# The recurrence's triangular inverse as two diagonal 64x64 blocks, the crossing step last, the pairs of heads written out

## The chip, the cores and the metric

The kernel runs on one core of a Trainium2 chip (trn2). Its engines are TensorE (matrix products, into the accumulator memory PSUM), VectorE, ScalarE, GpSimd and SyncE; in the profile PE, PEld (TensorE's weight loads), DVE, ACT, POOL and SP. They run beside each other and wait for each other through semaphores. The metric is the device time of one execution, in microseconds (us). All data is float32.

## The reference

Two networks in a row, on 256 tokens of width 1024. The change touches one step of the second one, the scan in its RWKV-7 mixer, which runs for 16 heads of width 64, forwards and backwards in time:

```python
def rwkv7_scan(r, w, k, v, kk, a):
    def step(state, inp):
        r_t, w_t, k_t, v_t, kk_t, a_t = inp
        sa = jnp.einsum('bhvk,bhk->bhv', state, -kk_t)
        state = (state * w_t[:, :, None, :] + sa[..., None] * (kk_t * a_t)[:, :, None, :]
                 + v_t[..., None] * k_t[:, :, None, :])
        return state, jnp.einsum('bhvk,bhk->bhv', state, r_t)
    ...
    _, out = lax.scan(step, jnp.zeros((nB, H, N, N), F32), xs)

    dir_out = []
    for d in range(2):
        ...
        o = rwkv7_scan(*ins)
        bonus = jnp.sum(rh * kd * r_k.astype(F32), axis=-1, keepdims=True) * vh
        dir_out.append((group_norm(o, gn_w, gn_b) + bonus.reshape(nB, S, D)) * g.astype(F32))
    y = dir_out[0] + dir_out[1]
```

`sa` of a token depends on the `sa` of all tokens before it. Over a chunk of 128 tokens that is a linear system whose matrix is the unit matrix plus a strictly triangular one, and the kernel solves it by inverting that matrix.

## The kernel before

The function `Rwkv.chunks` (from L2288 on) holds the whole recurrence. It works on pairs of heads: eight pairs, each 128 channels wide, `i` = 0 to 7. Within a pair there are two directions `d`, two chunks `t` of 128 tokens and two heads `hh`; the four matrices of one direction are numbered `n` = 2t + hh. Each direction has four banks of PSUM, `ps[:, 4 * d + 0..3, :]`. Every engine has its own program `pair(i)`, and `all_pairs` (L2347) writes the first and the last pair out and puts the six between into a loop (`Fori`), where slices are addressed and semaphores awaited through registers. Semaphores are named in `N`, and `wait(eng, name, i, k)` waits for the k-th signal of pair i.

A pair goes through these steps:

- *Products* (L2468, L2471). TensorE multiplies the scaled keys (`KR`, part of the tiles `used`) with `Bs` and `Ks`. VectorE multiplies the results by the masks `keep` and writes `GM` (L2673, eight instructions of 128x512); its part `GM[d][:, n, 0]` is the triangular matrix, transposed.
- *M1* (L2478) is the same matrix not transposed, from four more matmuls in a direction, masked by VectorE (L2681).
- *Inversion*. `Xi` is the inverse, `XT` its transpose, both 128x128 and at first the unit matrix (ScalarE, L2413, L2414). There are seven levels (`LEVELS`); level k doubles the size of the inverted diagonal blocks from 2^k. Level 0 is a masked copy of M1 into `Xi` and of GM into `XT` (L2687, L2688; `level` holds the places as 0 or 1). In levels 1 to 6 TensorE does the half step, `P = GM' Xi` (L2488), for both directions; ScalarE copies it out of PSUM (L2422, `Pb`, the same memory as `M1`, printed as M); TensorE makes `XT' P` (L2505) and `P' XT` (L2507); VectorE copies the new places of both (L2701, L2702). The last level makes only `XT`.
- *Gates*. In level 4 (`GATES_AT`) TensorE also makes the gates and the bonus (L2496, L2497), between the half step and the products.
- *State*. TensorE makes the right side `rhs`, ScalarE copies it (L2438), `XT' rhs` is `sa` (all these through `by_halves`, L136, in tiles of 128x64), then the chunk's state (L2538) and outputs. VectorE scales the state into `S0` (L2710), and the second chunk goes the same way. ScalarE copies the outputs `o` (L2450) and the next pair's `used` (L2409), on which the next pair's products wait.

VectorE and ScalarE do more beside the inversion, in an order that is written out. At the start of level 1, 2 and 3 VectorE runs two pieces of `output(i - 1)` (group norm and gates of the pair before, L2626 to L2658), at the start of level 4, 5 and 6 one piece of `factors(i + 1)` (L2580 to L2610, with the exponentials `exps` of ScalarE between), and the last piece after level 6, before it scales the state. GpSimd copies `v` into `vc` once in each pair (L2387), as soon as the pair before has ended.

## Time and profile before

| | us |
|---|---|
| median of 3 runs (3013.49 to 3015.53) | 3014.8 |
| the profiled execution | 3018.51 |
| its span, from the first to the last instruction | 3016.8 |
| TensorE busy | 2778.6 (92%) |
| VectorE busy | 784.0 (26%) |
| ScalarE busy | 420.1 (14%) |
| the mean granted clock of TensorE | 0.965 of 2.4 GHz |

The profile is one execution, recorded by instruction. Times in its views are counted from the start of the span. A float32 matmul stands in it as two records, each with a weight load of its own. A record's own duration contains the way through the array, so the pace of a group is read from the distance of starts. "PEclk" or the granted clock is 1.00 at 2.4 GHz and 0.50 at 1.2 GHz. The recurrence lies between 2282 and 2729 us.

### The profile page before, as it was taken

The numbers are of one execution on the slowest core, as the hardware profiler recorded it, in microseconds if no ns is written. First come the engines' busy times: TensorE is split into PE (matmuls) and PEld (weight loads), VectorE is DVE, ScalarE is ACT, GpSimd is POOL, SyncE is SP. The second block draws the span as 40 slices with busy tenths as digits, with TensorE's granted clock in tenths as the row PEclk, the third lists the DMA queues.
The fourth block names the chain that finished last, engine by engine and source line by source line (L and its number), as shares of the span: only waits on it lengthen the run. The fifth ranks groups of instructions, "written<-read, shape, count | busy, mean of one in ns | idle before, by whom it ended". The sixth has DMA issues, their size and how long they took to land. (4 is left out here: it accounts for less than half of the span.)

```text
span 3016.8 us, 73080 instructions
## 1 busy us (share of the span) xinstructions
PE 2778.6 (92%) x32601; PEld 2324.4 (77%) x32601; DVE 784.0 (26%) x1979; ACT 420.1 (14%) x927; POOL 84.5 (3%) x144
## 2 busy tenths in 40 slices
PE   8899999989889999999999977999998898897998
PEld 7677776768789999899899765666686788786665
DVE  5412000630211101101101112100426777873001
ACT  1101000111110101101001112100123323221000
POOL 0100000010000000000000000000000000001000
PEclk9899999989989999999999997999998999999999
DMA  7334445433379999999999930644410000001442
GB/s 216 112 127 133 147 152 161 136 98 112 147 303 407 407 407 407 407 407 407 407 407 407 319 126 21 187 152 158 152 56 4 3 2 3 2 2 64 153 153 97
DMA packets 291365, 571.04 MB, mean 189 GB/s; under 512 B 18182, under 2 KB 181764, under 8 KB 291284
## 3 DMA queue, kind: packets, MB, share of 16 engines
q1 hardware_dynamic: 291284, 569.92, 52.3%
q8 instruction: 56, 0.92, 0.1%
q14 instruction: 25, 0.20, 0.0%
HBM read 568.79 MB, written 5.28 MB: 190 GB/s over the span
## 5 line engine op out<-in xcount | busy, mean ns | idle before, releaser
L1737 PE MATMUL ps<-xg,ring 128*64 128x80 f32 x14336 | 519.6, 234 | 7.2 <-issue 2.2
L1737 PEld LDWEIGHTS ps<-xg,ring 128*64 128x64 f32 x14336 | 507.1, 138 | 18.0 <-DMA ring<-in_moe_w_up_dram 8.3
L1332 PE MATMUL ps<-xT,ring 128*128 128x256 f32 x1728 | 379.8, 379 | 6.1 <-PEq L452 3.0
L1332 PEld LDWEIGHTS ps<-xT,ring 128*128 128x128 f32 x1728 | 328.3, 190 | 67.0 <-issue 22.4
L1344 PE MATMUL ps<-ring,hidden 128*128 128x512 f32 x688 | 301.8, 592 | 0.0
L1753 PE MATMUL ps<-hidden,expert_down 128*64 128x80 f32 x7168 | 259.5, 233 | 9.2 <-DVE hidden L1829 4.8
L1753 PEld LDWEIGHTS ps<-hidden,expert_down 128*64 128x64 f32 x7168 | 251.9, 137 | 14.8 <-DVE hidden L1829 6.3
L1344 PEld LDWEIGHTS ps<-ring,hidden 128*128 128x128 f32 x688 | 130.9, 190 | 147.3 <-issue 145.3
L618 PE MATMUL ps<-ring,xT 128*128 128x256 f32 (+1 forms) x1056 | 228.3, 379 | 7.4 <-PEq L1213 4.1
L618 PEld LDWEIGHTS ps<-ring,xT 128*128 128x128 f32 x1056 | 198.6, 196 | 36.2 <-issue 9.7
L618 PE MATMUL ps<-xT,ring 128*128 128x256 f32 (+1 forms) x944 | 214.9, 390 | 10.2 <-PEq L596 4.5
L618 PEld LDWEIGHTS ps<-xT,ring 128*128 128x128 f32 (+1 forms) x944 | 178.1, 190 | 44.8 <-issue 14.8
L1829 DVE TENSOR_TENSOR hidden<-acted,ps 128x320 f32<-128x320 f32 x64 | 28.6, 446 | 676.2 <-PE ps L1737 676.2
L1392 DVE TENSOR_TENSOR hidden<-acted,ps 128x512 f32<-128x512 f32 x43 | 29.6, 688 | 605.2 <-ACT acted L1369 397.5
L2488 PE MATMUL ps<-Xi,GM 128*128 128x128 f32 x768 | 116.2, 298 | 18.8 <-DVE Xi L2687 8.9
L2488 PEld LDWEIGHTS ps<-Xi,GM 128*128 128x128 f32 x768 | 99.9, 203 | 32.7 <-DVE Xi L2701 19.8
L1791 ACT ACTIVATE acted<-ps 128x320 f32<-128x320 f32 x64 | 22.4, 401 | 627.0 <-PE ps L1737 627.0
L1369 ACT ACTIVATE acted<-ps 128x512 f32<-128x512 f32 x43 | 25.7, 597 | 598.5 <-PE ps L1332 598.5
L2507 PE MATMUL ps<-XT,M 128*128 128x128 f32 x768 | 102.9, 279 | 0.0
L2507 PEld LDWEIGHTS ps<-XT,M 128*128 128x128 f32 x768 | 95.6, 196 | 0.3
L2505 PE MATMUL ps<-M,XT 128*128 128x128 f32 x640 | 89.6, 286 | 0.0
L2422 ACT ACTIVATE M<-ps 128x512 f32<-128x512 f32 x96 | 57.3, 597 | 218.6 <-PE ps L2488 218.6
(361 smaller groups left out, 2455.9 us busy)
## 6 DMA issues: line engine op xcount, KB each, us to landing
ring<-in_moe_w_gate_dram SPq DMA_DIRECT2D x128, 896.0 KB, 16.6
ring<-in_moe_w_up_dram SPq DMA_DIRECT2D x128, 896.0 KB, 16.7
expert_down<-in_moe_w_down_dram SPq DMA_DIRECT2D x96, 1024.0 KB, 17.3
ring<-in_mlp_w_dram SPq DMA_DIRECT2D x64, 1024.0 KB, 5.7
ring<-in_w_xkv_dram SPq DMA_DIRECT2D x16, 1024.0 KB, 5.2
expert_down<-in_moe_w_down_dram SPq DMA_DIRECT2D x32, 512.0 KB, 16.5
ring<-in_ffn_w_gate_dram SPq DMA_DIRECT2D x11, 1024.0 KB, 5.4
ring<-in_ffn_w_up_dram SPq DMA_DIRECT2D x11, 1024.0 KB, 5.3
```

Of the source, the lines that this page charges most:

```text
L618: mm = pe.matmul(bank(n, dst), left(here), right(here), start=(i == 0), stop=(i == len(pairs) - 1))
L1332: mm = pe.matmul(bank[:, m * SEQ:(m + 1) * SEQ], w[:, c, m * P:(m + 1) * P], self.xT[:, c, :], start=(c == 0), stop=(c == KC - 1))
L1344: mm = pe.matmul(ps[:, 4 + 2 * t + half, :], hidden[:, p, f, t * P:(t + 1) * P], w[:, f, half * 512:(half + 1) * 512], start=first and f = ...
L1369: act.activation(acted[:, p, :], gb[p], ACT.Silu if up else ACT.Relu).then_inc(s["act_done"].sem, 1)
L1392: dve.tensor_tensor(hidden[:, p].rearrange("p f s -> p (f s)"), acted[:, p, :], ub[p], ALU.mult).then_inc(s["hidden_ready"].sem, 1)
L1737: mm = pe.matmul(bank[b][o:o + HEAD, at, :], w[:, c, f * P + o:f * P + o + HEAD], xg[:, p * E_STEP + c, :], start=(p == 0 and c == 0 and a ...
L1753: mm = pe.matmul(yT[c // 4][o:o + HEAD, c % 4, :], w[:, j, c * P + o:c * P + o + HEAD], hidden[:, f, :], start=False, stop=False, skip_gro ...
L1829: dve.tensor_tensor(hidden[:, part, :], acted[:, part, :], src, ALU.mult).then_inc(hidden_ready, 1)
L2422: act.activation(Pb[d][:].rearrange("p a b -> p (a b)"), ps[:, 4 * d, :], ACT.Copy).then_inc(q["half_ready"].sem, 1)
L2488: mm = pe.matmul(ps[:, 4 * d, n * P:(n + 1) * P], GM[d][:, n, 0, :], Xi[d][:, n, :], start=True, stop=True)
L2505: pe.matmul(ps[:, 4 * d + 1, n * P:(n + 1) * P], XT[d][:, n, :], Pb[d][:, n, :], start=True, stop=True)
L2507: mm = pe.matmul(ps[:, 4 * d + 2, n * P:(n + 1) * P], Pb[d][:, n, :], XT[d][:, n, :], start=True, stop=True)
```

## The change

- The inverse is held as its two diagonal blocks of 64x64. `XX[d]` [P, 4, 2, 64] has in the upper 64 partitions the first block and in the lower 64 the second, `XX[.., 0, :]` the inverse and `XX[.., 1, :]` its transpose. `LEVELS` is 6. Each matmul of the inversion becomes two, one for each block `b`, with rows, columns and output in the half `b`: tiles of 64x64 on the diagonal of the array.
- `M1` is made by 16 matmuls of 64x64 in a direction (both kinds, plain and transposed, of both blocks). ScalarE copies it and turns the sign; VectorE's masked multiplication is gone. What lies outside the places is not used.
- One masked copy of 128x512 in a level and direction serves both `XX` parts. ScalarE's copies of the half step have 256 columns.
- A crossing step joins the blocks at the end: four matmuls in a direction (`L2530` of the new kernel), a copy by ScalarE into `PI`, which has unit matrices beside it, four matmuls with 64x128 weights (L2536), a copy by VectorE into `XB`.
- `sa` takes the first half from a 64x64 tile of `XX` and the other from a 128x64 tile, `XB`.
- The third piece of `factors(i + 1)` runs after the last level, ahead of the copy of `XB`.
- All eight pairs are written out; there is no loop.

```diff
-LEVELS = 7
+LEVELS = 6
@@ all_pairs
-            pair(0, first=True)
-            with eng.Fori(1, pairs - 1) as i:
-                pair(i)
-            pair(pairs - 1, last=True)
+            for i in range(pairs):
+                pair(i, first=i == 0, last=i == pairs - 1)
@@ ScalarE
-                        act.activation(Xi[d][:], m.ident[:].unsqueeze(1).to_broadcast([P, 4, P]), ACT.Copy)
-                        act.activation(XT[d][:], m.ident[:].unsqueeze(1).to_broadcast([P, 4, P]), ACT.Copy).then_inc(q["x_begun"].sem, 1)
+                        act.activation(XX[d][:].rearrange("p n k e -> p (n k) e"), eyes[:].unsqueeze(1).to_broadcast([P, 8, HEAD]), ACT.Copy).then_inc(q["x_begun"].sem, 1)
                     for d in range(2):
+                        wait(act, "m1_done", i, d + 1)
+                        act.activation(M1[d][:].rearrange("p t h e -> p h t e"), ps[:, 4 * d:4 * d + 2, 0:4 * HEAD].rearrange("p h (t e) -> p h t e", t=TT),
+                                       ACT.Copy, scale=-1.0).then_inc(q["m1_ready"].sem, 1)
...
-                            act.activation(Pb[d][:].rearrange("p a b -> p (a b)"), ps[:, 4 * d, :], ACT.Copy).then_inc(q["half_ready"].sem, 1)
+                            act.activation(Pb[d][:].rearrange("p a b -> p (a b)"), ps[:, 4 * d, 0:4 * HEAD], ACT.Copy).then_inc(q["half_ready"].sem, 1)
...
+                    for d in range(2):
+                        wait(act, "cross_done", i, d + 1)
+                        to, other = half(1 - d), half(d)
+                        act.activation(PI[to, :, other], ps[to, 4 * d, 0:4 * HEAD].rearrange("p (n e) -> p n e", n=4), ACT.Copy).then_inc(q["cross_ready"].sem, 1)
                     if not last:
                         exps(i + 1, 1)
@@ TensorE
-                                mm = pe.matmul(ps[:, 4 * d + hh, t * P:(t + 1) * P], KR[d][half(hh), t, 0, :], Bs[d][half(hh), t, :], start=True, stop=True)
+                            for kind in range(2):
+                                for b in range(2):
+                                    for hh in range(2):
+                                        a, e = KR[d][half(hh), t, 0, half(b)], Bs[d][half(hh), t, half(b)]
+                                        at = (2 * t + kind) * HEAD
+                                        mm = pe.matmul(ps[half(b), 4 * d + hh, at:at + HEAD], e if kind else a, a if kind else e, start=True, stop=True)
...
                             for n in range(4):
-                                mm = pe.matmul(ps[:, 4 * d, n * P:(n + 1) * P], GM[d][:, n, 0, :], Xi[d][:, n, :], start=True, stop=True)
+                                for b in range(2):
+                                    h = half(b)
+                                    mm = pe.matmul(ps[h, 4 * d, n * HEAD:(n + 1) * HEAD], GM[d][h, n, 0, h], XX[d][h, n, 0, :], start=True, stop=True)
...
-                            if k < LEVELS - 1:
-                                for n in range(4):
-                                    pe.matmul(ps[:, 4 * d + 1, n * P:(n + 1) * P], XT[d][:, n, :], Pb[d][:, n, :], start=True, stop=True)
                             for n in range(4):
-                                mm = pe.matmul(ps[:, 4 * d + 2, n * P:(n + 1) * P], Pb[d][:, n, :], XT[d][:, n, :], start=True, stop=True)
+                                for kind in range(2):
+                                    for b in range(2):
+                                        h = half(b)
+                                        xt, p = XX[d][h, n, 1, :], Pb[d][h, n, :]
+                                        at = (2 * n + kind) * HEAD
+                                        mm = pe.matmul(ps[h, 4 * d + 1, at:at + HEAD], p if kind else xt, xt if kind else p, start=True, stop=True)
                             mm.then_inc(q["step_done"].sem, 1)
+                    for d in range(2):
+                        wait(pe, "x_ready", i, 2 * (LEVELS - 1) + d + 1)
+                        to, other = half(1 - d), half(d)
+                        for n in range(4):
+                            mm = pe.matmul(ps[to, 4 * d, n * HEAD:(n + 1) * HEAD], GM[d][other, n, 0, to], XX[d][other, n, 0, :], start=True, stop=True)
+                        mm.then_inc(q["cross_done"].sem, 1)
+                    for d in range(2):
+                        wait(pe, "cross_ready", i, d + 1)
+                        to = half(1 - d)
+                        for n in range(4):
+                            mm = pe.matmul(ps[:, 4 * d + 1, n * HEAD:(n + 1) * HEAD], PI[to, n, :], XX[d][to, n, 1, :], start=True, stop=True)
+                        mm.then_inc(q["block_done"].sem, 1)
...
                             for hh in range(2):
-                                mm = by_halves(pe, ps[:, 4 * d + 1, hh * HEAD:(hh + 1) * HEAD], XT[d][:, 2 * t + hh, :], rhs[d][:, hh, :], start=True, stop=True)
+                                cols, n = slice(hh * HEAD, (hh + 1) * HEAD), 2 * t + hh
+                                pe.matmul(ps[first_half, 4 * d + 1, cols], XX[d][first_half, n, 1, :], rhs[d][first_half, hh, :], start=True, stop=True)
+                                mm = pe.matmul(ps[other, 4 * d + 1, cols], XB[d][:, n, :], rhs[d][:, hh, :], start=True, stop=True)
@@ VectorE
-                            if lv < LEVELS - 1:
-                                dve.copy_predicated(Xi[d][:], ..., ps[:, 4 * d + 1, :]...).then_inc(q["xi_ready"].sem, 1)
-                            dve.copy_predicated(XT[d][:], ..., ps[:, 4 * d + 2, :]...).then_inc(q["x_ready"].sem, 1)
+                            dve.copy_predicated(whole(XX[d][:]), places(d, lv), ps[:, 4 * d + 1, :].rearrange("p (n e) -> p n e", n=4)).then_inc(q["x_ready"].sem, 1)
+                    beside(after, 1)
+                    for d in range(2):
+                        wait(dve, "block_done", i, d + 1)
+                        dve.tensor_copy(XB[d][:].rearrange("p n e -> p (n e)"), ps[:, 4 * d + 1, 0:4 * HEAD]).then_inc(q["block_ready"].sem, 1)
                     beside(after, 2)
```

How TensorE's program changes, first pair, from the last transpose before the inversion through level 1. Rows give the line, the operation, output and inputs, the output's shape and a count of matmuls; `M_214` and `M_215` are the half steps of the two directions. Before:

```order
L2481 MATMUL ps<-ident,Ks 128x128
L2488 MATMUL ps<-Xi,GM 128x128 x8
L2505 MATMUL ps<-M_214,XT 128x128 x4
L2507 MATMUL ps<-XT,M_214 128x128 x4
L2505 MATMUL ps<-M_215,XT 128x128 x4
L2507 MATMUL ps<-XT,M_215 128x128 x4
```

and of the changed kernel:

```order
L2495 MATMUL ps<-ident,Ks 128x128
L2504 MATMUL ps<-XX,GM 64x64 x16
L2523 MATMUL ps<-Pb,XX 64x64 x2
L2523 MATMUL ps<-XX,Pb 64x64 x2
L2523 MATMUL ps<-Pb,XX 64x64 x2
L2523 MATMUL ps<-XX,Pb 64x64 x2
```

Eight matmuls of the half step became sixteen smaller ones, and the sixteen of the products thirty-two (the two L2523 rows stand eight times in a level).

TensorE again, first pair, the end of the inversion and the first product with `rhs`. Before:

```order
L2488 MATMUL ps<-Xi,GM 128x128 x8
L2507 MATMUL ps<-XT,M_214 128x128 x4
L2507 MATMUL ps<-XT,M_215 128x128 x4
L136 MATMUL ps<-vc,GM 64x64 x8
L136 MATMUL ps<-rhs,XT 64x64 x8
L2538 MATMUL ps<-sa,rowsBK 64x64 x2
```

and of the changed kernel:

```order
L2530 MATMUL ps<-XX,GM 64x64 x8
L2536 MATMUL ps<-XX,PI 128x64 x8
L136 MATMUL ps<-vc,GM 64x64 x8
L2559 MATMUL ps<-rhs,XX 64x64
L2560 MATMUL ps<-rhs,XB 64x64
```

The seventh level went, the two parts of the crossing step came, and the product with `rhs` alternates between two kinds of tiles.

VectorE at the same place. Before:

```order
L2597 TENSOR_TENSOR Y<-X,ring 128x256
L2702 COPY_PREDICATED XT<-level,ps 128x512 x2
L2599 TENSOR_SCALAR fa<-ring,cc 128x256
L2600 SCALAR_TENSOR_TENSOR kd<-fa,k 128x256
L2601 TENSOR_TENSOR bb<-xT,ring 128x256
```

and of the changed kernel:

```order
L2727 COPY_PREDICATED XX<-level,ps 128x512 x2
L2623 SCALAR_TENSOR_TENSOR S<-ones,ring 128x128 x2
L2626 COPY MT<-S 128x2
L2627 TENSOR_TENSOR MT<-S 128x2
L2628 TENSOR_TENSOR X<-S 128x256
L2630 TENSOR_TENSOR Y<-X,ring 128x256
L2731 COPY XB<-ps 128x256 x2
L2632 TENSOR_SCALAR fa<-ring,cc 128x256
```

The third piece of the next pair's factors (up to Y) stood ahead of the last level's copies and stands behind them now, and `XB` lies between it and the fourth piece.

## Rows read from the trace of the kernel before

**Rows 1.** Groups of instructions, 2250 to 2800 us: busy us, mean ns | idle before, releasers.
```profile
L2701 DVE COPY_PREDICATED Xi<-level,ps 128x512 f32<-128x512 int32 x80 | 58.2, 728 | 59.8 <-PE ps L2507 56.5 <-DVE Ks L2610 2.1 <-DVE XT L2702 1.0
```

**Rows 2.** Timeline, level 2 of pair 2: start us, us, engine, instruction [idle before <-releaser].
```profile
2416.53 0.97 PEld L2488 LDWEIGHTS ps<-Xi,GM 128*128 128x128 f32 x8
...
2417.74 0.60 ACT L2422 ACTIVATE M<-ps 128x512 f32<-128x512 f32 x1 [4.99 <-PE ps L2488]
...
2422.66 0.73 DVE L2701 COPY_PREDICATED Xi<-level,ps 128x512 f32<-128x512 int32 x1 [0.32 <-PE ps L2507]
...
2423.44 0.97 PEld L2488 LDWEIGHTS ps<-Xi,GM 128*128 128x128 f32 x8 [1.07 <-DVE Xi L2701]
```

**Rows 3.** Timeline of GpSimd: its copy of v at the start of a pair.
```profile
2344.30 0.40 POOL L2387 COPY vc<-v 128x256 f32 x1 [61.54 <-PE ps L136]
...
2455.33 0.40 POOL L2387 COPY vc<-v 128x256 f32 x1 [41.10 <-PE ps L136]
...
2510.16 0.40 POOL L2387 COPY vc<-v 128x256 f32 x1 [40.68 <-PE ps L136]
...
2563.37 0.40 POOL L2387 COPY vc<-v 128x256 f32 x1 [39.06 <-PE ps L136]
...
2670.35 0.40 POOL L2387 COPY vc<-v 128x256 f32<-128x256 f32 x1 [38.96 <-PE ps L136]
```

**Rows 4.** Timeline: small tiles, and a copy of 256 columns.
```profile
2397.29 0.40 PE L136 MATMUL ps<-vc,GM 128*64 128x64 f32 x8
...
2397.52 1.00 PE L136 MATMUL ps<-rhs,XT 128*64 128x64 f32 x16
...
2399.25 0.38 ACT L2450 ACTIVATE o<-ps 128x256 f32<-128x256 f32 x1 [0.41 <-PE ps L136]
...
2403.91 0.71 PE L2478 MATMUL ps<-Bs,used 64*128 64x128 f32 x8
...
2404.56 0.33 PE L2481 MATMUL ps<-ident,Bs 128*128 128x128 f32 x1
```

**Rows 5.** VectorE by stretches: stretch, its length, busy (x), PEclk, DMA share, GB/s.
```profile
2410.48:2412.63 2.15, 1.84 (x17) 0.50 0.00 0
2418.28:2422.35 4.07, 3.66 (x13) 1.00 0.00 0
2425.12:2428.21 3.09, 2.90 (x13) 1.00 0.00 0
2438.40:2441.61 3.21, 2.93 (x9) 1.00 0.00 0
2444.40:2446.19 1.79, 1.72 (x7) 1.00 0.00 0
2284.35:2287.35 3.00, 2.93 (x9) 0.50 0.01 4
```

**Rows 6.** Timeline of VectorE: state of pair 2, GM of pair 3.
```profile
2450.79 1.43 DVE L2710 TENSOR_SCALAR S<-ps,used 64x64 f32<-64x64 f32 x4
2456.63 4.88 DVE L2673 TENSOR_TENSOR GM<-ps,keep 128x512 f32<-128x512 f32 x8 [4.41 <-PE ps L2471]
```

**Rows 7.** Stretches, all engines: length, PE, PEld, DVE, ACT, POOL, PEclk, DMA, GB/s.
```profile
2405.00:2406.00 1.00, 0.00 (x0) 0.00 (x0) 1.00 (x3) 0.38 (x1) 0.00 (x0) 1.00 0.00 0
2408.00:2409.00 1.00, 1.00 (x5) 1.00 (x6) 1.00 (x3) 0.00 (x0) 0.00 (x0) 0.50 0.00 0
```

**Rows 8.** Timeline: the first GM products, the last matmul of the recurrence.
```profile
2292.02 4.87 DVE L2673 TENSOR_TENSOR GM<-ps,keep 128x512 f32<-128x512 f32 x8
...
2722.68 0.29 PE L136 MATMUL ps<-vc,GM 128*64 128x64 f32 x4
```

**Rows 9.** Timeline and stretches in an earlier stage, around 950 us.
```profile
948.61 1.34 PE L1712 MATMUL ps<-zeros 1*128 1x320 f32 x4
...
949.00:950.00 1.00, 1.00 (x5) 0.48 (x4) 0.41 (x1) 0.00 (x0) 0.00 (x0) 1.00 1.04 414
950.00:951.00 1.00, 1.00 (x12) 0.67 (x13) 0.42 (x1) 0.00 (x0) 0.00 (x0) 0.51 1.01 400
```

64 lines of the change are left out of this document (30 added, 34 removed).

## The prediction

> **What bounds the kernel now.** The change touches one stage, the recurrence of the last mixer: eight pairs of heads in a row, 2288 to 2723 us of a span of 3016.8 us. I read its groups of instructions first [rows 1]. Before VectorE's masked copies (L2701) there are 59.8 us idle, 56.5 of them for the matmuls of L2507. So TensorE is what the inversion waits for. The timeline of one level says the same [rows 2]: 8 weight loads of 128 columns take 0.97 us, about 0.11 each with the matmul behind it. A level has 8 for each of three products in each of two directions, 48 x 0.111 = 5.3 us, and the level shown lasts from 2416.53 to 2423.44 = 6.9 us, since VectorE's other work (below) held it up. Of a pair, the length is read from GpSimd, which copies v once in each [rows 3]: pairs 1 to 6 take (2670.35 - 2344.30) / 6 = 54.3 us, the shortest, 2510.16 to 2563.37, 53.2.
>
> **What a 64x64 tile costs.** No row has one. The nearest are the 128x64 tiles behind L136 [rows 4]: 8 instructions start within 2397.29 to 2397.52, 0.029 us each, two tiles of the array working side by side. Tiles of 64 rows do that too: L2478, 64 rows by 128 columns, has 8 in 0.71 us with the last one's 0.27, some 0.06 each instead of 0.11. The new code alternates the two diagonal quadrants, which differ in rows and in columns. I take 0.029 us. The bounds: 0.025 (the same row, no better) and 0.058, if the two quadrants do not overlap.
>
> **One level, after.** Instructions in a direction: 8 matmuls, 16 records, for the half step (0.46 us), 16 matmuls, 32 records, for the two products (0.93). Both directions: 2.8 us instead of 5.3. But a level is also a chain. ScalarE's copy of the half step has 256 columns and not 512, 0.38 us [rows 4] instead of 0.60 [rows 2]; VectorE's copies are one of 512 instead of two, 0.73 [rows 2]. An engine takes up a finished copy 0.05 us later (2422.66 + 0.73 to 2423.44). For one direction: 0.46 + 0.22 (the last record, as 0.40 less seven starts in rows 4) + 0.05 + 0.38 + 0.05 + 0.93 + 0.22 + 0.05 + 0.73 + 0.05, about 3.2 us. Levels that are alone therefore last 3.2 us, not 2.8.
>
> **And VectorE has other work in them.** It finishes the pair before (levels 1 to 3) and prepares the next (from level 4), and I took the length of each piece from the trace [rows 5]: 2.15, 4.07, 3.09 us, then 3.21 and 1.79; the last piece, as long as the fourth, takes 2.9 from 2447.88 to the row at 2450.79 [rows 6]. Two masked copies follow each piece, 0.62 + 0.73 = 1.35 us with the pipelining that the rows show. This is the new bound. I count a middle pair from K, the end of the eight GM products, to the next K; that of pair 3 is 2456.63 + 4.88 = 2461.51 [rows 6], 6.2 us behind its copy of v at 2455.33 [rows 3], and I use the same 6.2 for the others.
> - Level 0: TensorE's first products M1 are now 16 matmuls in a direction (0.93 us) instead of 4, and ScalarE copies them (0.60) where VectorE multiplied by the mask. VectorE is rid of that multiplication, but waits for the second direction: copies end at K + 2.6.
> - Level 1: 2.15 + 1.4: K + 6.2. Level 2: 4.07 + 1.35: K + 11.6. Level 3: 3.09 + 1.35: K + 16.0.
> - Level 4: here TensorE has the gates as well (8 matmuls of 128 columns, 1.8 us), and it is the bound: K + 21.2.
> - Level 5: 3.21 + 1.35: K + 25.75. There is no level 6.
> - Behind it: 1.79 us of the next pair's work, K + 27.55. Meanwhile the crossing step runs: 8 records for each direction in one quadrant (0.46), ScalarE's copy (0.38), 8 records with 64x128 weights (0.9, as L2488 with its 128 columns). It is ready about when VectorE is, so XB ends at K + 28.4; then 2.9 us: the state's scaling begins at K + 31.3.
> - From there to the next K: 2461.51 - 2450.79 = 10.7 us [rows 6], unchanged except for the product with rhs: it now alternates 64x64 and 128x64 tiles. Changing the tile's shape costs something like the step from L2478 to L2481 (0.71 us of records, 0.27 of them the last's, and 0.65 until the next shape starts [rows 4]: 0.1 more than its pace). Four in each direction are 0.8 us.
> - The loop is written out: VectorE's pieces have register work in it. The fourth piece takes 3.00 us in the first pair, which is straight code already, and 3.21 in the loop [rows 5]; with 0.1 to 0.2 for a piece I take 0.7 off a pair. What else it costs (more instructions to be fetched) I put at nothing: the last pair is straight code as well, and L136 keeps its pace there.
>
> Sum: 31.3 + 10.7 + 0.8 - 0.7 = 42.1 us, if the clock stays at 2.4 GHz.
>
> **The clock.** In the middle of a pair TensorE falls to 1.2 GHz: from 2405 to 2406 it had nothing to do, from 2408 on the granted clock is 0.50 [rows 7], for some microseconds, in six of the eight pairs. Of the six middle ones four have it, and the mean is 1.1 us above the shortest, which has none [rows 3]: 1.7 us for one. After the change TensorE has larger gaps: 2.8 us of work in levels of 4.4 to 5.4, and about 2 us of nothing before VectorE frees the crossing step's followers. At 1.2 GHz a level needs 2 x 2.8 = 5.6 us, and a fall that lasts one to two levels costs about 2.3 us at the start of the pair and some 2.5 at its end (cross and block steps twice as long, with the state behind them). I take 0.75 of the first, 0.4 of a fall in levels 2 and 3 (1.5) and 0.6 of the last: 3.8 us. A middle pair: 42.1 + 3.8 = 45.9, a gain of 8.4.
>
> **The ends.** Pair 0, from K = 2292.02 + 4.87 = 2296.9 [rows 8] to pair 1's at 2344.30 + 6.2 = 2350.5, takes 53.6. It has no pair before it, so levels 1 to 3 take 3.2 us each; by the same steps 27.3 + 11.5 + 3 = 41.8, a gain of 11.8. Pair 7 has nothing to prepare: from K = 2670.35 + 6.2 to the last matmul (2722.68 + 0.29, rows 8) 46.4 us; after, 16.0 at level 3, 21.2 at 4, 24.4 at 5 (3.2 more), 1.9 for the crossing (0.38 + 0.9 + the copy and the waits between), 6.2 for the rest as from the last masked copy to the end now, 0.8 and 2 for the clock: 35.3, a gain of 11.1. All else (loads of tables, the copies of the unit matrices) lies far ahead or beside idle engines. Together 6 x 8.4 + 11.8 + 11.1 = 73.3 us. The profiled execution took 3018.5 us (its span 3016.8), so 2945.2; the median of the runs is 3.7 us lower: **2941 us**.
>
> **A rule against it.** L2478's two row halves write different banks of PSUM. The new diagonal quadrants write one bank, in different partitions; no row shows row tiles doing that. The Trainium skill, TensorEngine Tiling (Array Packing), Restrictions and Gotchas, says of this that "Different row tiles cannot access same PSUM bank simultaneously". By that rule 0.058 us would hold, and the time would be that of the first rival, 3006 us, instead of 2941; the trace has no row that bears it out or speaks against it.
>
> **Rivals.**
> - *No overlap on the diagonal.* 0.058 us an instruction makes a level 96 x 0.058 = 5.6 us, what it is now. One level less and the half of the last save 2.7, the crossing step and M1 give it back: a pair of about 53.4 against 54.3, seven or eight us in all, and the last pair as before: 3006 us; with 1 us either way in a pair, 2998 to 3014.
> - *The clock stays low (slower).* Other rows speak for it: the slice from 949 to 950 is all busy, first with a tile of one row (L1712, 1x128), and so is the next, but its clock is 0.51 [rows 9]. So what the tile covers may count, and 64x64 tiles, two at a time, cover half the array. The Trainium skill, TensorE: Matmul & The Clock Gate, Part 1, speaks of how busy the engine has been recently; by that alone slices of 1.00 would have kept 2.4 GHz, and this rival would have no ground. Against it: 128x64 tiles in rows 4 ran at full clock, with the array full. If the inversion runs at 1.2 GHz from K to the state's scaling, levels take 5.7 us, the gates 3.6, the crossing step 5.4: 43 us instead of 31.3, the tail 12.5: 55.5 against 54.3. Pairs 0 and 7 lose 2 and 1.5: about +10 us, 3025. It decides from the point where more than about 80% of the inversion is at 1.2 GHz.
> - *The instructions are not there in time.* A pair in straight code has about 790 matmul records, twice that with the weight loads. Were each matmul late by 0.01 us where TensorE bounds, a fifth of them, 1.6 us a pair and 13 us in all would go: 2954 us. The last pair shows no such gap, so I give it little.
>
> **Chances.** Forecast 0.70 (2913 with no fall at all, 8 x 3.5 us less; 2981 with two falls more, 5 us, in every pair); no overlap 0.09; low clock 0.17 (3005 to 3045); the rest 0.04. The range 2908 to 3018 takes in the first, nearly all of the second and the low edge of the third. A measurement of this kernel can tell about 0.2%, 6 us, from no change: faster 0.75, within 0.07 (half of no overlap, the edge of the low clock), slower 0.18.
>
> **What would show it.** In the profile after: the spacing of L2523's records (0.029 right, 0.058 the first rival); VectorE busy most of a pair (above 0.8) and TensorE idle for it in levels 1 to 3, with GpSimd's copies of v 42 to 48 us apart; level 4 alone bound by TensorE; one fall of the clock more in each pair at the crossing step. Wrong it would be if the granted clock were 0.5 through most of the inversion, or if L2559 and L2560 cost more than 0.5 us in a direction.

## The result and the profile after

The changed kernel takes 2949.7 us (median of 4 runs, 2943.2 to 2952.2) where the kernel before takes 3015.2 beside it: a ratio of 0.978, 95% interval 0.9763 to 0.9797. Forecast were 2941 us, in a range of 2908 to 3018. The profiled execution took 2948.8 us (span 2947.0), 69.7 less than the 3018.5 of before; the forecast from it was 73.3.

Three groups of the page after. The columns are as in [rows 1]: busy us, mean ns of one | idle time before, and what ended it.

```profile
L2504 PE MATMUL ps<-XX,GM 64*64 64x64 f32 x1280 | 54.8, 228 | 29.4 <-DVE XX L2727 23.5
L2523 PE MATMUL ps<-Pb,XX 64*64 64x64 f32 x1280 | 80.6, 224 | 0.0
...
L2504 PEld LDWEIGHTS ps<-XX,GM 64*64 64x64 f32 x1280 | 44.7, 137 | 39.4 <-DVE XX L2727 30.0
```

Before, VectorE's masked copy waited 56.5 us for TensorE [rows 1]. The group that answers to it, VectorE from 2250 to 2800 us after, waits 28.6:

```profile
L2727 DVE COPY_PREDICATED XX<-level,ps 128x512 f32<-128x512 int32 x80 | 55.8, 722 | 32.2 <-PE ps L2523 28.6 <-DVE Ks L2643 1.2 <-DVE o L2674 1.2
```

Most of what is left of that wait is level 4, with the gates: the two copies of pair 1 there, below, wait 1.92 + 0.20 us; eight times that is 17 us. In the other direction TensorE's half step now waits 23.5 us for VectorE. Both waits are there, and in different levels, as the prediction had it.

GpSimd's copy of v, as in [rows 3], at the start of pairs 1 and 7:

```profile
2332.75 0.40 POOL L2389 COPY vc<-v 128x256 f32<-128x256 f32 x1 [50.44 <-PE ps L136]
...
2609.48 0.40 POOL L2389 COPY vc<-v 128x256 f32<-128x256 f32 x1 [33.51 <-PE ps L136]
```

(2609.48 - 2332.75) / 6 = 46.1 us for a middle pair, against 54.3 before and 45.9 forecast. Now pair 1 in VectorE's timeline (start, us, instruction; as in [rows 6]):

```profile
2334.16 4.87 DVE L2706 TENSOR_TENSOR GM<-ps,keep 128x512 f32<-128x512 f32 x8 [6.06 <-PE ps L2481]
...
2343.29 1.55 DVE L2727 COPY_PREDICATED XX<-level,ps 128x512 f32<-128x512 int32 x2
2348.74 1.34 DVE L2727 COPY_PREDICATED XX<-level,ps 128x512 f32<-128x512 int32 x2 [0.17 <-DVE o L2674]
2352.90 1.33 DVE L2727 COPY_PREDICATED XX<-level,ps 128x512 f32<-128x512 int32 x2
2358.08 0.73 DVE L2727 COPY_PREDICATED XX<-level,ps 128x512 f32<-128x512 int32 x1 [1.92 <-PE ps L2523]
2359.02 0.73 DVE L2727 COPY_PREDICATED XX<-level,ps 128x512 f32<-128x512 int32 x1 [0.20 <-PE ps L2523]
2362.80 1.33 DVE L2727 COPY_PREDICATED XX<-level,ps 128x512 f32<-128x512 int32 x2 [0.17 <-DVE Ks L2643]
...
2366.84 0.42 DVE L2731 COPY XB<-ps 128x256 f32<-128x256 f32 x1 [0.47 <-PE ps L2536]
2371.58 0.70 DVE L2738 TENSOR_SCALAR S<-ps,used 64x64 f32<-64x64 f32 x2 [1.40 <-PE ps L2571]
...
2380.58 4.87 DVE L2706 TENSOR_TENSOR GM<-ps,keep 128x512 f32<-128x512 f32 x8 [7.02 <-PE ps L2481]
```

K is 2334.16 + 4.87 = 2339.03. Read off against the prediction's own marks, in us behind K; the last column is pair 1 of the experiment "fill" below, whose clock never falls (its rows stand there):

| end of | forecast at full clock | after, pair 1 | fill, pair 1 |
|---|---|---|---|
| level 1 | 6.2 | 5.8 | 5.8 |
| level 2 | 11.6 | 11.1 | 11.1 |
| level 3 | 16.0 | 15.2 | 15.2 |
| level 4 | 21.2 | 20.7 | 20.8 |
| level 5 | 25.75 | 25.1 | 25.2 |
| XB | 28.4 | 28.2 | 27.9 |
| state's scaling begins | 31.3 | 32.6 | 30.8 |
| next K | 42.1 | 46.4 | 42.7 |

Up to XB the pair is as drawn. From there to the next K it takes 18.2 us (46.4 - 28.2), where 13.7 were drawn at full clock and fill has 14.8. Two views show why. First the product that gives sa, TensorE's timeline of pair 2, at half clock (step 0, for the first chunk: the first three rows) and at full clock (step 1, for the second: the last three, with the very last record):

```profile
2414.74 0.47 PE L2559 MATMUL ps<-rhs,XX 64*64 64x64 f32 x2
2415.15 0.47 PE L2560 MATMUL ps<-rhs,XB 128*64 128x64 f32 x2
2415.55 0.47 PE L2559 MATMUL ps<-rhs,XX 64*64 64x64 f32 x2
...
2421.46 0.33 PE L2559 MATMUL ps<-rhs,XX 64*64 64x64 f32 x2
2421.72 0.33 PE L2560 MATMUL ps<-rhs,XB 128*64 128x64 f32 x2
...
2423.36 0.22 PE L2560 MATMUL ps<-rhs,XB 128*64 128x64 f32 x1
```

Two records of one shape, then the other shape: 0.257 us each time at full clock, 0.40 at half. Eight of these are a step of both directions: 2.06 or 3.2 us, where its 16 records at 0.029 would be 0.47. From the first to the last start step 1 takes 2423.36 - 2421.46 = 1.90 us. Second, the granted clock (length, busy PE, PEld, DVE, ACT, POOL, then PEclk, DMA, GB/s; as in [rows 7]): pair 1 from K to the end of XB, its end, and level 3 of pair 2:

```profile
2339.03:2367.26 28.23, 22.78 (x572) 20.97 (x574) 23.30 (x76) 8.36 (x24) 2.40 (x4) 0.98 0.03 7
...
2366.00:2376.00 10.00, 10.00 (x112) 8.66 (x111) 5.01 (x14) 2.64 (x10) 0.00 (x0) 0.50 0.01 2
2397.00:2400.00 3.00, 3.00 (x62) 3.00 (x62) 2.81 (x10) 0.43 (x2) 0.00 (x0) 0.50 0.00 0
```

The clock falls to 1.2 GHz at the end of all eight pairs, for 7 to 10 us, and in levels 2 and 3 of pairs 2, 4 and 6, for 3 to 4 us; never at the start of a middle pair. TensorE is busy all the time in the last two rows, and works at half speed there. Ahead of these two falls it was not: it was busy for 8.5 of the 10 us up to 2365.5 and for 7.0 of the 10 us up to 2396.5.

Last, the spacing on which the forecast hung, TensorE in level 1 of pair 2:

```profile
2388.34 0.28 PE L2523 MATMUL ps<-Pb,XX 64*64 64x64 f32 x4
2388.46 0.28 PE L2523 MATMUL ps<-XX,Pb 64*64 64x64 f32 x4
```

Four records in 0.117 us: 0.029 each. All of them write one bank of PSUM, the two quadrants to different partitions.

### The profile page after: what moved, and what is told of

Same layout as the page of the kernel before. It is cut to its first block and busy times, and to the rows that moved or that the text cites. A ratio compares the mean times of both kernels' runs of the same rounds, so it can differ in the third digit from the quotient of the medians.

```text
span 2947.0 us, 76608 instructions
## 1 busy us (share of the span) xinstructions
PE 2700.9 (92%) x34905; PEld 2243.5 (76%) x34905; DVE 708.9 (24%) x1851; ACT 400.6 (14%) x929; POOL 84.5 (3%) x144
## 5 line engine op out<-in xcount | busy, mean ns | idle before, releaser
L2504 PE MATMUL ps<-XX,GM 64*64 64x64 f32 x1280 | 54.8, 228 | 29.4 <-DVE XX L2727 23.5
L2523 PE MATMUL ps<-Pb,XX 64*64 64x64 f32 x1280 | 80.6, 224 | 0.0
L2523 PE MATMUL ps<-XX,Pb 64*64 64x64 f32 x1280 | 79.7, 223 | 0.0
L397 POOL TENSOR_SCALAR stat<-stat 128x1 f32<-128x1 f32 x32 | 14.3, 447 | 2165.3 <-ACT junk L392 1702.0
L2504 PEld LDWEIGHTS ps<-XX,GM 64*64 64x64 f32 x1280 | 44.7, 137 | 39.4 <-DVE XX L2727 30.0
L836 DVE SCALAR_TENSOR_TENSOR conv<-gated,cols,conv 128x256 f32<-128x256 f32 x180 | 71.4, 473 | 0.0
```

Source lines behind the costliest of these rows:

```text
L836: ins = dve.scalar_tensor_tensor(conv[:, i, :], gated[:, i, k:k + SEQ], w, conv[:, i, :], ALU.mult, ALU.add)
L2504: mm = pe.matmul(ps[h, 4 * d, n * HEAD:(n + 1) * HEAD], GM[d][h, n, 0, h], XX[d][h, n, 0, :], start=True, stop=True)
L2523: mm = pe.matmul(ps[h, 4 * d + 1, at:at + HEAD], p if kind else xt, xt if kind else p, start=True, stop=True)
```

## The experiments

Each starts from the changed kernel unless said otherwise, and is timed in turns with the kernel before. The changed kernel is 2949.7 us throughout; times are medians, ratios are against the kernel before. "K to K" is the length of a pair as above.

**1. The quadrants one after the other (serial).**

```diff
-                            for n in range(4):
-                                for b in range(2):
+                            for b in range(2):
+                                for n in range(4):
                                     h = half(b)
```
and the same exchange in the loops of L2523.

> The changed kernel with the matmuls of L2504 and L2523 in another order alone: all of one diagonal block, then all of the other, so that tiles that follow each other are the same quadrant. Same arithmetic, same number of instructions. If the gain came from the overlap of the two quadrants (0.029 us a record in the trace after), the spacing becomes 0.058, a level has 5.6 us of matmuls instead of 2.8, levels 1, 2, 3 and 5 take 5.6 and level 4 about 7.5: some 7 us more in a pair, 3000 to 3010 us. If 64x64 tiles are short in any order (the columns alone set the time), the spacing stays 0.029 and the time 2950.

2990.1 us, ratio 0.9931 (0.9906 to 0.9955). TensorE's timeline, in level 2:

```profile
2355.01 0.28 PE L2523 MATMUL ps<-Pb,XX 64*64 64x64 f32 x2
2355.13 0.28 PE L2523 MATMUL ps<-XX,Pb 64*64 64x64 f32 x2
...
2355.36 0.28 PE L2523 MATMUL ps<-XX,Pb 64*64 64x64 f32 x2
2355.48 0.33 PE L2523 MATMUL ps<-Pb,XX 64*64 64x64 f32 x4
```

Two records in 0.117 us: 0.058 each, twice the spacing, with the same arithmetic and the same bank. So it is the alternation of quadrants that makes the tiles short, not their size: of the 65 us of the change 40 hang on the order of two loops. The time came out 10 to 20 us better than I expected. Here and there (the x4 row) records of the two blocks start within one another after all; a direction's 32 records took 1.50 us, 0.047 each, and not 1.86. Middle pairs are 51.0 us from K to K, 4.9 longer, where 7 were expected. In pair 1 levels 1, 3 and 4 are 1.4, 1.0 and 1.6 us longer, level 5 is 0.5, and level 2 stays at 5.2: there VectorE's work still takes longer than the slower tiles.

**2. and 3. The product that gives sa (sa_grouped, sa_full).** Grouped:

```diff
                             for hh in range(2):
                                 cols, n = slice(hh * HEAD, (hh + 1) * HEAD), 2 * t + hh
                                 pe.matmul(ps[first_half, 4 * d + 1, cols], XX[d][first_half, n, 1, :], rhs[d][first_half, hh, :], start=True, stop=True)
+                            for hh in range(2):
+                                cols, n = slice(hh * HEAD, (hh + 1) * HEAD), 2 * t + hh
                                 mm = pe.matmul(ps[other, 4 * d + 1, cols], XB[d][:, n, :], rhs[d][:, hh, :], start=True, stop=True)
```

> The changed kernel with the product that gives sa in another order: the two 64x64 products of a direction (L2559), then the two 128x64 ones (L2560), so that the tile's shape changes twice in a direction and not four times. In the trace after, two records of one shape take 0.257 us before the next shape starts (2421.46 to 2421.72) at full clock and 0.40 (2414.74 to 2415.15) at half. If the change of shape costs (0.257 less 2 x 0.058 = 0.14 each), four of eight go: 0.6 us in step 1, 0.8 in step 0, 1.4 us a pair, about 2938 us. If the cost is only that two records of one shape are the same quadrant, it stays: 2950.

2936.6 us, ratio 0.9731 (0.9711 to 0.975): 13 us better than the changed kernel, 11.7 expected. In step 1 of pair 1 four records of one shape start 0.37 us ahead of the next shape (2371.90 to 2372.27), which is 4 x 0.058 and 0.14 for the change. Full:

```diff
+                        act.activation(XF[d][half(d)], XX[d][half(d), :, 1, :], ACT.Copy).then_inc(q["first_ready"].sem, 1)
...
+                                wait(pe, "first_ready", i, d + 1)
...
-                                pe.matmul(ps[first_half, 4 * d + 1, cols], XX[d][first_half, n, 1, :], rhs[d][first_half, hh, :], start=True, stop=True)
+                                pe.matmul(ps[first_half, 4 * d + 1, cols], XF[d][:, n, :], rhs[d][:, hh, :], start=True, stop=True)
```

> The changed kernel with no 64x64 tile in the product that gives sa: ScalarE copies the block behind the last level into a 128x64 tile whose other rows are zero (XF, two copies of 64 rows in a pair, 0.38 us each, beside the crossing step), and L2559 uses it with all rows, so that its tiles and L2560's are two column halves in turn, as L136's are. 32 records then take 0.029 at full clock (0.47 us for a step of both directions) where the trace after has 2.06 (8 x 0.257) in step 1 and 3.2 (8 x 0.40, half clock) in step 0. If this is what the change lost against my sum, a pair gets 1.6 + 2.3 = 3.9 us shorter: 2918 us. If my sum's 0.8 us a pair was right and the trace's groups are drawn out by something else (waits for ScalarE), 2943.

2919.7 us, ratio 0.9676 (0.9657 to 0.9695): 30 us better, 32 expected. TensorE's timeline in step 1:

```profile
2370.92 0.27 PE L2565 MATMUL ps<-rhs,XF 128*64 128x64 f32 x1
2370.93 0.27 PE L2566 MATMUL ps<-rhs,XB 128*64 128x64 f32 x1
2371.03 0.22 PE L2565 MATMUL ps<-rhs,XF 128*64 128x64 f32 x1
2371.04 0.22 PE L2566 MATMUL ps<-rhs,XB 128*64 128x64 f32 x1
```

The tiles start in pairs, one of each half, 0.01 us apart. A direction's eight records start within 0.23 us, the 16 of both within 0.76, since the second direction starts 0.3 us behind the first; my 0.47 had no such gap. Of one half of the tiles half the rows are zeros, so this kernel computes more and is faster. Two things changed here: the shape stays the same, and neighbours now lie in different halves of the array and run side by side. Grouping, which changes the number of shape changes alone, gave 13 of the 30 us. The falls at the ends of the pairs are shorter too, 4 to 7 us and not 7 to 10.

**4. Nothing idle (fill).** Matmuls of the unit matrix into a bank that is free there, behind levels 1, 2 and 5.

```diff
+                def fill(count):
+                    for _ in range(count):
+                        pe.matmul(ps[:, 2, 0:P], m.ident[:], m.ident[:], start=True, stop=True)
...
                             mm.then_inc(q["step_done"].sem, 1)
+                        fill((0, 8, 4, 0, 0, 5)[k])
```

> The changed kernel with full 128x128 matmuls of the unit matrix into an unused bank where TensorE waits for VectorE: 8 behind level 1 (gap of 2.29 us), 4 behind level 2 (1.13), 5 behind level 5 (1.46), at 0.22 us each. They fill waits and are on no path. If the falls of the granted clock at each pair's end (6.8 to 10.2 us at 0.50) come from the idle and the small tiles ahead of them, they get fewer or shorter; matmuls that bound there run at twice the pace and a pair gets 1 to 4 us shorter: 2920 to 2942. If the falls come from the crossing step and the product for sa themselves, behind the fillers, the clock falls as before and the time is 2950 (or up to 3 more, where a filler is in the way).

2939.8 us, ratio 0.9743 (0.9724 to 0.9763): 10 us better by doing more. Four of the seven pairs from 0 to 6 kept a fall, three had none and are 42.7 us. Pair 0 is 4.2 us longer than in the changed kernel (46.8 and 42.6): it has two falls, and VectorE has no work of a pair before it in levels 1 to 3, so there the fillers are on the path. Pair 1 is all at the full clock:

```profile
2345.80:2388.50 42.70, 39.61 (x822) 35.18 (x822) 32.35 (x97) 14.04 (x40) 2.79 (x5) 1.00 0.02 6
```

and VectorE's timeline of it:

```profile
2344.53 1.28 DVE L2711 TENSOR_TENSOR GM<-ps,keep 128x512 f32<-128x512 f32 x2
...
2355.52 1.34 DVE L2732 COPY_PREDICATED XX<-level,ps 128x512 f32<-128x512 int32 x2 [0.18 <-DVE o L2679]
2359.69 1.35 DVE L2732 COPY_PREDICATED XX<-level,ps 128x512 f32<-128x512 int32 x2
...
2365.83 0.73 DVE L2732 COPY_PREDICATED XX<-level,ps 128x512 f32<-128x512 int32 x1 [0.20 <-PE ps L2527]
2369.62 1.34 DVE L2732 COPY_PREDICATED XX<-level,ps 128x512 f32<-128x512 int32 x2 [0.17 <-DVE Ks L2648]
2372.76 0.96 DVE L2736 COPY XB<-ps 128x256 f32<-128x256 f32 x2
2376.56 1.43 DVE L2743 TENSOR_SCALAR S<-ps,used 64x64 f32<-64x64 f32 x4
2383.63 4.88 DVE L2711 TENSOR_TENSOR GM<-ps,keep 128x512 f32<-128x512 f32 x8 [5.64 <-PE ps L2485]
```

K is 2344.53 + 1.28 = 2345.81. The state's scaling follows XB's 2373.72 by 2.84 us, VectorE's piece, so at full clock the first product for sa is hidden behind that piece; in the kernel after, at half clock, it is not (4.3 us, of which VectorE waits 1.40 for L2571). The falls cost a middle pair 46.1 - 42.7 = 3.4 us.

**5. Both (combo),** with 5 more fillers in the gap of level 0.

> sa_full and fill together, and 5 more fillers between the two directions of level 0 (a gap of 1.60 us before the second L2492 in the trace after). In the trace of fill, pairs without a fall of the clock last 42.7 us from K to K; sa_full takes 1.6 off step 1, which is on the path, and nothing off step 0, which at full clock lies beside VectorE's last piece (the state's scaling begins at K + 30.7, XB and the 2.9 us piece behind it). So 41.1 us a pair when no pair has a fall: 2908 us, against 2920 for sa_full alone, whose pairs last 42.5 on average. If the falls stay as frequent as in fill (4 of 8 pairs), 2912 to 2916. If the two gains were the same microseconds (sa_full's gain was only a shorter fall), 2920.

2917.2 us, ratio 0.967 (0.9657 to 0.9682). Between 2300 and 2600 us one fall is left, and six pairs are 41.5 us from K to K, as expected to 0.4. But the time is 9 us above the 2908. More than half of that lies inside the stage. I had 1.4 us less than sa_full in each of eight pairs, 11 in all. In the profiled executions the six middle pairs gain 1.0 each, since sa_full's are 42.5 on average and combo's 41.5, and the last gains 1.3 (33.8 us from K to the last matmul of the recurrence, and 35.1). Pair 0 is 1.1 us longer: VectorE has no work of a pair before it there, and the fillers are in the way (level 2 ends at K + 10.97, in sa_full at K + 9.30). That makes 6 of the 11 us. Two more stretches of the profiled execution differ. Ahead of the first pair, in code that is the same, its clock is 0.89 where that of sa_full and of the changed kernel is 1.00, and the first K comes 5 us later than sa_full's. And behind the last pair, where TensorE has little to do, the clock is low for 17 us, 10 in sa_full:

```profile
2240.00:2270.00 30.00, 26.82 (x113) 21.84 (x112) 9.73 (x25) 14.78 (x36) 0.00 (x0) 0.89 0.00 1
2627.00:2644.00 17.00, 7.91 (x26) 6.76 (x27) 8.21 (x29) 1.19 (x2) 1.75 (x3) 0.51 0.47 162
```

The first I put to the test with the same kernel run once more, since four of the five kernels with fillers showed it in their profiled execution and none of the others did.

> The kernel combo once more, for one look. In its profiled execution the clock was 0.89 from 2240 to 2270 us, in code ahead of the change, and the first K came 5 us later than in sa_full (2300.9 and 2295.9). Of the five kernels with fillers, four show this and one (combo_gn_state) does not; none of those without fillers does. If it belongs to the program (its length or place in memory moves something ahead of the stage), it is there again: 0.89 and a first K near 2300. If it is chance of an execution, it need not be: 1.00 and 2296 or so, and the whole about 5 us shorter.

2916.4 us, span 2914.6, and the stretch now reads

```profile
2240.00:2270.00 30.00, 25.66 (x124) 20.22 (x123) 10.24 (x29) 17.19 (x45) 0.00 (x0) 1.00 0.00 1
```

with the first K at 2296.2. So the fall there, worth 4 to 5 us, does not come in every execution of this program; whether fillers make it likelier stays open (four of six profiled executions with fillers have it, none of the eight without). The low stretch behind the last pair is there again (14 us). That it takes back a part of the gain is not shown: from the last matmul of the recurrence to the end of the span it is 293.4 us in combo, 293.1 in combo_again and 291.3 in sa_full, but the kernels without fillers alone range from 290.9 (lean) to 294.5 (sa_grouped), with 293.5 in the changed kernel.

**6. What the fillers must be (fill64).** Combo's fillers in one 64x64 quadrant, twice as many.

```diff
-                        pe.matmul(ps[:, 2, 0:P], m.ident[:], m.ident[:], start=True, stop=True)
+                        pe.matmul(ps[0:HEAD, 2, 0:HEAD], m.ident[0:HEAD, 0:HEAD], m.ident[0:HEAD, 0:HEAD], start=True, stop=True)
...
-                        fill((0, 8, 4, 0, 0, 5)[k])
+                        fill((0, 16, 8, 0, 0, 10)[k])
```

> combo with fillers of 64x64 in one quadrant of the array instead of 128x128: twice as many (20 beside level 0 and level 5 in all, 16 and 8 in levels 2 and 3), 0.116 us each instead of 0.22, so TensorE is busy for the same time at the same places. If the clock goes by how busy TensorE is, the trace looks like combo's: one fall between the pairs' K, 41.5 us a pair, 2917 us. If it goes by how much of the array works, the falls stay as in sa_full (one or two in each pair, 42.5 us a pair on average): 2920 or some more. The trace is to tell these apart, since the times are close: count the stretches with a granted clock of 0.50 between 2300 and 2600 us (1 in combo, 12 in sa_full).

2917.6 us, ratio 0.9674 (0.966 to 0.9687). Five falls between 2300 and 2600 us. Combo has one, combo_again too, and sa_full, with no fillers, has ten there (the 12 of the expectation counted two behind 2600). From the first K to the last TensorE is busy for 274 of 292 us here and for 270 of 291 in combo. So neither reading holds alone: with TensorE as busy, fillers that cover a quarter of the array left more falls than full ones did, and fewer than there are with no fillers. These are counts of one execution each, of two for combo's kernel. In time fill64 and combo are the same.

**7. VectorE's work in level 2 left out (lean).** The subtraction of the mean, the scaling and the two products with the norm's weights are not computed.

```diff
-                        for n in range(4):
-                            ins = ts(ov[:, n, :], ov[:, n, :], mv[d][:, n, 0:1], rs[d][:, 1, n:n + 1], ALU.subtract, ALU.mult)
-                        link(ins)
-                        o2 = o[d][:].rearrange("p (t e) -> p t e", t=TT)
-                        link(tt(o2, o2, gn[:, 0:1, columns(j)].to_broadcast([P, TT, P]), ALU.mult))
-                        link(tt(o2, o2, gn[:, 1:2, columns(j)].to_broadcast([P, TT, P]), ALU.add))
```

> The changed kernel without the middle part of the output's work on VectorE (L2670 to L2674: subtracting the mean, scaling and the two products with the norm's weights are left out, so the output is another), the 4.1 us that stand in level 2. If VectorE is the new bound there, level 2 lasts as in pair 0, which has no such work (5.81 to 9.30 = 3.5 us), and not 5.2: seven pairs shorter by 1.7, 2938 us. If TensorE still bounds the levels, 2950. Were all of the 4.1 us on the path, 2921.

2930.8 us, ratio 0.9727 (0.971 to 0.9745). VectorE's timeline, levels 1 and 2 of pair 1:

```profile
2342.43 1.55 DVE L2721 COPY_PREDICATED XX<-level,ps 128x512 f32<-128x512 int32 x2
2345.91 1.56 DVE L2721 COPY_PREDICATED XX<-level,ps 128x512 f32<-128x512 int32 x2 [1.93 <-PE ps L2523]
```

Level 2 is 3.5 us and ends with a wait for TensorE; of 4.1 us of VectorE's work left out, 1.7 come back. VectorE is the bound of that level, and TensorE stands 1.7 us behind it. Expected were 2938. Of the 7 us more, 5 lie behind the last K, where I had counted 1.7: from it to the end of the span it is 324.4 us instead of 331.2. Of these 6.8 us 4.2 lie ahead of the last matmul: 1.7 are level 2, and the rest goes with a fall of the clock that pair 7 has in the changed kernel and not here. The other 2.6 lie behind it, where the last pair's output lacks the whole piece; how much of them is that piece is not shown.

**8. and 9. Writing out.** The loop over pairs 1 to 6 on all engines but TensorE:

```diff
+            if loop:
+                pair(0, first=True)
+                with eng.Fori(1, pairs - 1) as i:
+                    pair(i)
+                pair(pairs - 1, last=True)
+                return
             for i in range(pairs):
...
-                all_pairs(pe, pair)
+                all_pairs(pe, pair, loop=False)
```

> The changed kernel with the loop over pairs 1 to 6 kept on every engine but TensorE, whose code stays written out. In the kernel before, writing out took 1.0 us off a pair without a fall of the clock (53.2 to 52.2 from K to K), in VectorE's levels 2 and 3 and in what follows; there VectorE was not the bound of most levels. Here it is, so the loop should cost as much or more: 1.0 to 1.5 us in each of six pairs, 2956 to 2959 us, with level 2 at 5.4 or more instead of 5.2. If writing out counted only where TensorE's own code was in the loop, 2950.

2957.4 us, ratio 0.9815 (0.9802 to 0.9829), and pairs 2 to 6 are 47.7 us from K to K. Not all of that is the loop's own work: each of these five pairs has a fall in levels 2 and 3 and one of 10 us at its end, where the changed kernel has the first in three pairs, and a shorter one behind it. In pair 1, which has only the fall at its end in both, it is 47.3 and 46.4 us. And the kernel before, written out, with nothing else changed:

```diff
-            pair(0, first=True)
-            with eng.Fori(1, pairs - 1) as i:
-                pair(i)
-            pair(pairs - 1, last=True)
+            for i in range(pairs):
+                pair(i, first=i == 0, last=i == pairs - 1)
```

> The kernel before with its pairs written out and nothing else changed. VectorE does not bound most levels there, TensorE does; its pieces are 0.1 to 0.2 us shorter, which counts only in levels 2, 3 and 5: 0 to 0.7 us a pair, 3010 to 3014 us. If writing out were a large part of what the change brought, it would be below 3000.

3007.4 us (11 runs), ratio 0.9974 (0.9964 to 0.9983). Two K's of VectorE's timeline:

```profile
2499.70 4.87 DVE L2671 TENSOR_TENSOR GM<-ps,keep 128x512 f32<-128x512 f32 x8 [4.41 <-PE ps L2469]
2551.93 4.88 DVE L2671 TENSOR_TENSOR GM<-ps,keep 128x512 f32<-128x512 f32 x8 [4.41 <-PE ps L2469]
```

52.2 us where the shortest pair of before has 53.2, so the loop costs 1.0 us in a pair without a fall; in the changed kernel it costs 7.7 us in six pairs, 1.3 each with the falls, 0.9 with the same fall in both. Of the change's 65 us, some 8 are the writing out, with what it does to the clock.

**10. and 11. On from there (combo_gn, combo_gn_state).** The norm's weights go to GpSimd:

```diff
-                        link(ins)
-                        o2 = o[d][:].rearrange("p (t e) -> p t e", t=TT)
-                        link(tt(o2, o2, gn[:, 0:1, columns(j)].to_broadcast([P, TT, P]), ALU.mult))
-                        link(tt(o2, o2, gn[:, 1:2, columns(j)].to_broadcast([P, TT, P]), ALU.add))
+                        s.do(ins)
...
+                        pool.tensor_tensor(o2, o2, gn[:, 0:1, columns(j)].to_broadcast([P, TT, P]), ALU.mult).then_inc(q["rstd_step"].sem, 1)
+                        wait(pool, "rstd_step", j, d + 3)
+                        pool.tensor_tensor(o2, o2, gn[:, 1:2, columns(j)].to_broadcast([P, TT, P]), ALU.add).then_inc(q["gn_rstd"].sem, 1)
```

> combo with the four products with the norm's weights (L2673, L2674, 0.46 us each on VectorE) given to GpSimd, which is idle there, and without the 8 fillers of level 1. VectorE has 2.0 us in level 2 then and not 4.1, so TensorE's chain bounds it: 3.5 us (as in lean) instead of 5.2, seven pairs shorter by 1.7, 2917 - 12 = 2905 us. Rival: GpSimd is slower on 128x256 than the 0.8 us an operation that leaves level 3 alone (its copy of this size takes 0.40), and VectorE waits for it in level 3: a gain of 0 to 6, 2911 to 2917. If two engines at work at once slow each other, VectorE's masked copies would take longer than 0.73.

2905.4 us, ratio 0.964 (0.9627 to 0.9653), as expected, but not pair by pair: the middle pairs without a fall are 40.3 us, 1.15 less than in combo and not 1.7, and pair 0 is 1.7 us shorter (39.8 and 41.5), since the fillers of level 1 are gone. GpSimd's two groups, and VectorE's L2688 and masked copies beside them, 2330 to 2620 us:

```profile
L2390 POOL TENSOR_TENSOR o<-o,gn 128x256 f32<-128x256 f32 x16 | 12.1, 758 | 1.3
L2388 POOL TENSOR_TENSOR o<-o,gn 128x256 f32<-128x256 f32 x16 | 11.7, 730 | 6.8 <-DVE o L2688 5.8
...
L2743 DVE COPY_PREDICATED XX<-level,ps 128x512 f32<-128x512 int32 x70 | 48.3, 721 | 20.8 <-PE ps L2539 18.8 <-DVE Ks L2661 1.0
...
L2688 DVE TENSOR_SCALAR o<-o,mv,rs 128x64 f32<-128x64 f32 x64 | 21.6, 411 | 0.7 <-POOL rs L2384 0.7
```

The masked copies, which read PSUM, stay at 721 ns. The subtraction and scaling, from SBUF to SBUF, takes 411 ns on average, against 309 in the changed kernel. The average hides what happens: the shortest, median and longest of the 64 are 301, 308 and 726 ns (in the changed kernel 299, 310 and 316). So most of them are as fast as ever, and a few last about as long as one of GpSimd's. Level 2 is 3.85 us and not 3.5, without a wait for TensorE ahead of its copies, and level 3, where L2698's mean goes from 276 to 321 ns and its longest is 764, is 0.2 us longer. Then the state's scaling ahead of VectorE's last piece:

```diff
-                    beside(after, 2)
                     for d in range(2):
                         wait(dve, "state_done", i, d + 1)
...
                         ins.then_inc(q["s0_ready"].sem, 1)
+                    beside(after, 2)
```

> combo_gn with the state's scaling (L2738) ahead of VectorE's last 2.9 us piece and not behind it. In pair 7 of combo, which has no such piece, the scaling begins at K + 29.43, in the others at K + 30.75: 1.3 us of waiting for VectorE. The piece then lies beside TensorE's second step, 11 us long; ScalarE takes its results only after the outputs. Seven pairs shorter by 1.3: 9 us less than combo_gn, 2896. If the piece's results are late for the next pair's first product, or the shorter pair lets the clock fall again, nothing: as combo_gn.

2897.7 us (2896.4 to 2902.9), ratio 0.9617 (0.9604 to 0.963). The scaling begins 1.0 us earlier in a pair (K + 28.6), and the pairs without a fall are 39.3 us; 2896 were expected. This is 52 us faster than the changed kernel and 116 faster than the one before.

The changed kernel with the loop on all engines, TensorE too, was planned and has no result, so what the loop would cost on TensorE stays open.

## Why the prediction held, step by step

- **A tile costs 0.029 us.** Right: 0.029 in the trace, the value I took, and 0.058 in most rows of serial, my bound for quadrants that do not overlap. (The other bound, 0.025, stands in no row.) The rule of the Trainium skill (TensorEngine Tiling (Array Packing), Restrictions and Gotchas), by which different row tiles do not reach one bank at once, did not hold here: the two diagonal quadrants wrote one bank in different partitions at 0.029 us each.
- **VectorE is the new bound, TensorE only in level 4.** Right. Lean shows it for level 2; in pair 1 the copies of levels 1, 3 and 5 follow VectorE's own work with no wait for TensorE. It is busy 23.3 of the 28.2 us from K to XB (0.83), but only 32.4 of the whole 46.4 (0.70), below the 0.8 that I had named for most of a pair. The levels end 0.4 to 0.8 us ahead of my marks. From level 3 on that is the writing out: in pair 1 of loop_but_pe level 3 ends at K + 15.7 and level 5 at 25.9. The 0.4 us of level 1 is there with the loop too.
- **Writing out, 0.7 us a pair.** 1.0 in the kernel before, 0.9 here in pair 1, and 1.3 on average with the falls that came with the loop. Somewhat too small. The rival of late instructions had no ground: L2523 keeps its pace.
- **The change of shape, 0.8 us a pair.** This is the term that failed, and my own mark for it (more than 0.5 us in a direction) was passed: 1.03 us at full clock, 1.6 at half. I had taken the price from one step between two shapes in [rows 4], as 0.1 us, and reckoned that the tiles would otherwise run side by side. Both were wrong. The row itself gives 0.15: L2478's last record starts 0.44 us behind its first, the next shape 0.65, and a step of its pace is 0.06. And the tiles don't run side by side: two records of one shape in turn are the same columns and wait for each other (2 x 0.058), and each change costs 0.257 - 0.117 = 0.14. Grouping saved what that says. At full clock only step 1 is on the path: 1.90 us from its first to its last start, 0.75 before [rows 4], so 1.15 more, where I had 0.8. For step 0 I had put nothing, which holds at full clock (fill) and not at half: there the scaling waits 1.40 us for TensorE.
- **The clock, 3.8 us a pair.** 3.4 measured, but elsewhere; that the size came out was luck. The largest part I had at the start of the pair (0.75 falls, 1.7 us), then 0.6 falls at its end (1.5) and 0.4 in levels 2 and 3 (0.6). There is none at the start in a middle pair, three in six in levels 2 and 3 (level 3 ends 0.9 us later in these pairs), and one in every pair at the end, where it costs most: 18.2 us from XB to the next K in pair 1 against 14.8 in fill. The product for sa stands in that stretch and is drawn out by the fall, to 3.2 us in step 0, so the errors of this term and the last one meet in one place.
- **The ends.** Pair 0 gained 11.0 (11.8 forecast). Pair 7 gained 8.6 (11.1): it lasts 37.7 us and not 35.3, from K to the end of the last matmul. The product for sa is where it went: sa_grouped's last pair lasts 37.0 us, sa_full's 35.1. VectorE's last piece, which covers a part of that product in the others, is not there. The two ends of it, VectorE's row and TensorE's:

```profile
2610.89 4.87 DVE L2706 TENSOR_TENSOR GM<-ps,keep 128x512 f32<-128x512 f32 x8 [5.83 <-PE ps L2481]
...
2653.20 0.28 PE L136 MATMUL ps<-vc,GM 128*64 128x64 f32 x3
```
 All pairs: 69 of the 73.3 us.

So the number was right to 0.3%, 8.7 us. A middle pair came out 0.2 us longer than forecast, because errors met: against fill's pair 1 the sum at full clock was 0.2 short up to the state's scaling (30.6, with the 0.7 for the writing out taken off, and 30.8) and 0.4 short behind it (11.5 and 11.9, mostly step 1 for sa), and the falls cost 0.4 less. The ends are 3.3 us of the miss. The profiled execution is off by 3.6 us in all (2945.2 and 2948.8). The rest of the 8.7 is the 3.7 us that I took off for the median of the runs: the changed kernel's profiled execution is 1 us below its median, not above. Taken without the clock, the forecast was 42.1 for 42.7.

**The rivals.** "No overlap on the diagonal" is what serial built: 2990 us, where I had 3006: the order lets some records overlap after all, and serial left M1's order as it was. "The clock stays low" did not come: most of the inversion ran at full clock. But its ground was sound in part. The clock stayed at 1.2 GHz from 2366 to 2376 us with TensorE busy all the time, though ahead of that fall it had waits, and what the fillers cover made a difference between combo and fill64. The Trainium skill (TensorE: Matmul & The Clock Gate, Part 1) speaks of how busy the engine has been; with TensorE busy for 270 of 291 and 274 of 292 us, full fillers left one fall and quarter ones five, so in these executions busy time alone does not tell it.

## What to carry to other kernels

The small tiles here were fast only next to a tile in another part of the array: write the loops so that neighbours in the program lie in different rows and columns, or in different column halves, and look at the spacing of records to see whether it worked. Keep one tile shape through a dependent stretch, even if that means multiplying by zeros. When work leaves TensorE, ask at once what the granted clock will do in the gaps, and look for what the engine that binds next could give away. Count the first and last round of a pipeline by themselves: here the fillers cost time in pair 0, where there was no gap to fill.
